# First block of a two-block network on one NeuronCore: raw products at the start of three stages, with the norm's root applied afterwards, and the state loaded in two parts

## The reference, cut to what matters

```python
def rms_norm(x, w):
    xf = x.astype(jnp.float32)
    y = xf * lax.rsqrt(jnp.mean(xf * xf, axis=-1, keepdims=True) + EPS)
    return (y * w.astype(jnp.float32)).astype(x.dtype)
def swiglu(x, w_gate, w_up, w_down):
    return (jax.nn.silu(x @ w_gate) * (x @ w_up)) @ w_down
```

## Time and profile before

| | |
|---|---|
| runs | 2658.94 us median of 3 (2658.17 to 2671.31) |
| the profiled execution | 2659.51 us |
| its span, first to last instruction | 2657.7 us |
| PE matmuls busy | 2567.2 us, 97% |
| PE weight loads busy | 2278.7 us, 86% |
| DVE busy | 1668.7 us, 63% |
| ACT busy | 1105.1 us, 42% |
| POOL busy | 66.1 us, 2% |
| DMA | 380.44 MB, mean 143 GB/s |

### The profile page before, as it was taken

The page is one execution under the profiler, slowest core; times in us unless marked ns, Lnnn a source line. Parts: engine busy times, 40 slices in busy tenths (PEclk is TensorE's granted clock), DMA queues, the critical chain, the costliest instruction groups (busy, mean ns, idle before and its releaser), DMA issues.

```text
span 2657.7 us, 38440 instructions
## 1 busy us (share of the span) xinstructions
PE 2567.2 (97%) x15728; PEld 2278.7 (86%) x15728; DVE 1668.7 (63%) x2629; ACT 1105.1 (42%) x1720; POOL 66.1 (2%) x60
## 2 busy tenths in 40 slices
PE   7998898999999999999999999999999999998998
PEld 7998798999888888778888888889888888888998
DVE  6767645777677665656644777655555446776655
ACT  5446654555322224444243422224222225655553
POOL 0001031000000000000000000000000000010000
PEclk9999999999999999999999999999999999999999
DMA  7775202675555543112222455553444423244554
GB/s 260 234 233 183 83 17 68 208 238 178 167 182 186 177 144 100 58 40 72 96 90 84 135 185 179 177 170 113 136 140 139 133 97 133 84 132 157 178 192 148
DMA packets 109536, 380.44 MB, mean 143 GB/s; under 512 B 11952, under 2 KB 15792, under 8 KB 108976
## 3 DMA queue, kind: packets, MB, share of 16 engines
q1 hardware_dynamic: 108352, 372.80, 42.6%
q10 hardware_dynamic: 1008, 5.18, 0.5%
HBM read 376.88 MB, written 1.05 MB: 142 GB/s over the span
## 4 chain that ended last, share of the span: by engine, by line
PE 89%; DVE 5%; ACT 3%; issue 2%; DMA 0%; SPq 0%; ACTq 0%; DVEq 0%
PE B L1497 26%; PE B L1498 25%; PE B L1499 25%; DVE w_lo L2126 2%; ACT w_hi L1819 1%; PE B L1758 1%; PE B L1741 1%; PE B L1512 1%; PE B L1651 1%; PE B L1513 1%; PE B L1664 1%; PE B L1514 1%; PE B L1748 1%; DVE AC L2371 1%; DVE TMP L2153 0%
## 5 line engine op out<-in xcount | busy, mean ns | idle before, releaser
L1497 PE MATMUL B<-U,w_hi 128*128 128x256 f32 (+1 forms) x2896 | 958.3, 331 | 7.7 <-DVE w_lo L2126 7.5
L1498 PE MATMUL B<-U,w_hi 128*128 128x256 f32 (+1 forms) x2896 | 950.1, 328 | 0.0
L1499 PE MATMUL B<-U,w_lo 128*128 128x256 f32 (+1 forms) x2896 | 950.0, 328 | 0.0
L2126 DVE TENSOR_TENSOR w_lo<-w_raw,w_hi 128x1024 fp32r<-128x1024 f32 (+3 forms) x583 | 683.6, 1185 | 391.9 <-ACT w_hi L1819 391.2
L1819 ACT ACTIVATE w_hi<-w_raw 128x1024 fp32r<-128x1024 f32 (+3 forms) x583 | 590.2, 1018 | 491.8 <-PE B L1499 470.4
L1497 PEld LDWEIGHTS B<-U,w_hi 128*128 128x128 f32 x2896 | 545.6, 188 | 64.3 <-issue 7.4
L1498 PEld LDWEIGHTS B<-U,w_hi 128*128 128x128 f32 x2896 | 545.5, 188 | 52.4 <-issue 1.5
L1499 PEld LDWEIGHTS B<-U,w_lo 128*128 128x128 f32 x2896 | 545.5, 188 | 51.9
L1497 PE MATMUL B<-HHf,w_hi 128*128 128x256 f32 (+1 forms) x1122 | 363.8, 324 | 1.7 <-DVE w_lo L2126 1.6
L1499 PE MATMUL B<-HHf,w_lo 128*128 128x256 f32 (+1 forms) x1122 | 362.9, 323 | 0.0
L1498 PE MATMUL B<-HLf,w_hi 128*128 128x256 f32 (+1 forms) x1122 | 362.9, 323 | 0.0
(11 more groups left out here) (355 smaller groups left out, 2537.9 us busy)
## 6 DMA issues: line engine op xcount, KB each, us to landing
w_raw<-in_w SPq DMA_DIRECT2D x504, 512.0 KB, 4.2
w_ada<-in_w SPq DMA_DIRECT2D x144, 512.0 KB, 3.3
w_raw<-in_w SPq DMA_DIRECT2D x58, 384.0 KB, 3.4
w_raw<-in_w SPq DMA_DIRECT2D x8, 320.0 KB, 2.8
X<-in_x SPq DMA_DIRECT2D x2, 1024.0 KB, 9.7
w_raw<-in_w SPq DMA_DIRECT2D x8, 256.0 KB, 2.7
BW<-in_bias ACTq DMA_DIRECT2D x1, 1536.0 KB, 10.3
K<-in_consts ACTq DMA_DIRECT2D x2, 640.0 KB, 4.5
```

The lines of the kernel that those rows point to most:

```text
L1497: pe.matmul(o, hi, xh, start=i == 0 and s.start, stop=False)
L1498: pe.matmul(o, hi, xl, start=False, stop=False)
L1499: e = pe.matmul(o, lo, xh, start=False, stop=i == last and s.stop)
L2126: dve.tensor_tensor(w_lo[:, plan.slot[u], 0:n], w_raw[:, plan.ring[u], 0:n], w_hi[:, plan.slot[u], 0:n].bitcast(F32), ALU.subtract).then_i ...
```

## The change

At the start of the three stages of the first block, four products instead of two are made side by side in two pairs, and they read `x w` without the root ("raw"). New step `raw`: ACT multiplies a tile of X by its gain into the high part, DVE makes the low part by one operation. It is done tile by tile as soon as the tile of X is final: after the load in the first FFN, after each `x_add` of the first FFN's down product for mixing, and after each `x_add1` of the output projection for the second FFN (in a new buffer `UR`; else in the free half of `U0`, `UO`). `raw_begin` then orders: the first half of the first pair (tiles 0 to 3, 24 matmuls), the sum over partitions and the root, the second half of the first pair (24), the second pair (48). The root comes in on evacuation: in `ffn_h` for columns 0 and 1 DVE multiplies the gate's product by r, ACT applies SiLU, DVE multiplies by r again and then by the up product; in `conv_in` for tiles 0 to 3 DVE multiplies by r while it copies. `norm_to_u` still makes the normalized state, which the next product (column tile 2 of an FFN; q0 in mixing) is the first to read. In `mix1`'s list, c2 and c3 move up behind c1. The state is loaded in two halves, with the first weight unit between them.

```diff
-                while done < min(at + AHEAD + 1, len(cut)) and (done < NH or cut[done - NH] in used):
+                while done < min(at + (s.n if s.kind == "fetch" and s.n else AHEAD + 1), len(cut)) and (done < NH or cut[done - NH] in used):
...
+    def raw_begin(self, name, view, keys, wts, stat):
+        need = tuple(("ul", ("raw", name, k)) for k in range(8))
+        b = [self.PS.get() for _ in range(4)]
+        f = dict(x=view, n=256, need=need)
+        self.add("pair", key=(), wts=wts[0][:8], b=b[0], b2=b[1], **f)
+        rb = stat.rsqrt(D)
+        self.add("pair", key=keys[:2], wts=wts[0][8:], k0=4, b=b[0], b2=b[1], **f)
+        self.add("pair", key=keys[2:], wts=wts[1], b=b[2], b2=b[3], **f)
+        return rb, dict(zip(keys, b))
...
-        order = "c0 c1 q0 q4 v b0 b1 o0 c2 c3 q1 q5 b2 b3 o1 c4 c5 c6 c7 s0 s1 q2 q6 b4 b5 o2 u0 u1 u2 u3 k0 k1 q3 q7 b6 b7 o3 c8 c9 c10 c11 s2 d w0 w1 g0 g1"
+        order = "c0 c1 c2 c3 q0 q4 v b0 b1 o0 q1 q5 b2 b3 o1 c4 c5 c6 c7 s0 s1 q2 q6 b4 b5 o2 u0 u1 u2 u3 k0 k1 q3 q7 b6 b7 o3 c8 c9 c10 c11 s2 d w0 w1 g0 g1"
...
+            elif k == "raw":
+                act.activation(HI[s.x][:, s.key[1], 0:256], X[:, s.key[1], 0:256], ACT.Copy,
+                               scale=col(*s.key)).then_inc(*up("uh", ("raw", *s.key)))
...
+            elif k == "raw":
+                dve.scalar_tensor_tensor(out=LO[s.x][:, s.key[1], 0:256], in0=X[:, s.key[1], 0:256], scalar=col(*s.key),
+                                         in1=HI[s.x][:, s.key[1], 0:256].bitcast(F32), op0=ALU.mult,
+                                         op1=ALU.subtract).then_inc(*up("ul", ("raw", *s.key)))
+            elif k == "conv_in" and s.rb:
+                dve.tensor_tensor(CV[:, s.key, 2:258], PS(s.b, 256), RB(s.rb, 256), ALU.mult).then_inc(*up("conv_r", s.key))
...
+                if s.rb:
+                    dve.tensor_tensor(h, PS(s.b, s.n), RB(s.rb, s.n), ALU.mult).then_inc(*up("g_r", s.key))
...
+                if s.rb:
+                    dve.tensor_tensor(h, h, RB(s.rb, s.n), ALU.mult).then_inc(*up("h_r", s.key))
...
-        sp.dma_start(X[:, :, 0:256], xs[:, :, 0:256]).then_inc(*landed("x", 0))
+        sp.dma_start(X[:, 0:4, 0:256], xs[:, 0:4, 0:256]).then_inc(*landed("x", 0))
         sp.dma_start(PC[:, 0:ncol], cols).then_inc(*landed("cols", 0))
+        weight_in(plan.cut[0])
+        sp.dma_start(X[:, 4:8, 0:256], xs[:, 4:8, 0:256]).then_inc(*landed("x1", 0))
+        weight_in(plan.cut[1])
         sp.dma_start(C1[:], consts[:, 0:256]).then_inc(*landed("c1", 0))
-        for u in plan.cut[:NR]:
-            sp.dma_start(w_raw[:, plan.ring[u], 0:plan.units[u][1]], source(u)).then_inc(*landed(f"w{plan.ring[u]}", u))
+        for u in plan.cut[2:NR]:
+            weight_in(u)
```

107 lines of the change are left out of this document (70 added, 37 removed).

## The result

| | before | changed |
|---|---|---|
| median of the runs | 2665.12 us of 4 | 2695.82 us of 4 (2691.30 to 2696.91) |
| ratio, 95% interval | | 1.0111 [1.0084, 1.0137] |
| profiled execution, its span | 2659.51, 2657.7 us | 2691.30, 2689.5 us |

The change costs 1.1%. In a second comparison it came out at 1.0096 [1.0059, 1.0133]. The forecast of 2674 had the sign right and the size at half, and the measured median lies outside its range of 2655 to 2685.

What follows compares the result with a forecast made beforehand. PE was taken to be nearly always busy, so only its stops and slow clock at the three stage starts could be won. 9.3 + 3 + 2.6 = 14.9 on 2659.5 gave 2674 us, range 2655 to 2685.

Steps and rivals of the forecast that it cites:

- the wait for `w_lo` in the value product: Sign of being right: in mixing, PE waits several us for the split's low part in the value product.
- First FFN, +9.3 forecast: Up product of column 3 starts at 46.5 instead of 37.2; +7.1 all at fast clock, +12.8 all slow.
- Mixing, +3 forecast: Value product ends at 237.2 where 233.2 is level, +4.0; 1 may come back behind; bounds -2 and +7.
- Three units from there, 8.2: Mixing: from the split of the value product's second unit at 229.0, three units take 8.2 us, to 237.2.
- my mark: Mixing: end of the value product, 227.76 before, taken as a point where PE runs without a stop again; level at 233.2.
- I have counted slow clock only in the first FFN: Clock assumption: slow products priced in the first FFN alone, none in the estimates for mixing or second FFN.
- Output projection and second FFN, +2.6 forecast: Column 3's up product in the second FFN starts at 488.2 against 485.65; bounds +0.5 and +5.3 (48 products slow).
- for two tiles and a split it then needs 3.3: Output projection: DVE needs 3.3 us where PE takes 2.7, so the second FFN's sum comes 1.2 late.
- The level case: Rival, chance 0.26, 2661 us: mixing bound by DVE and ACT chains, early taps give time back; mixing -5, first FFN +7.
- The faster case: Rival, chance 0.13, 2643 us: norm gets done under the second pair at all three places; -16.
- The rival of the clock that stays up: Rival, chance 0.12, 2672 us: pair products keep the clock through the sum; 7.1 + 3 + 2.6.
- The worse one: Rival, chance 0.07, 2688 us: POOL's stretch slows DVE's attention work, some 6 us over mixing's estimate, plus slow clock behind all norms.

Runs made afterwards that it cites:

- b4_parts: Kernel before with the state loaded in two parts, the first weight unit between them, no raw products: 2663.48 us, ratio 0.9990.
- c2_cb_early: Changed kernel with the loads of CN and CB right behind mixing's root, BW left behind the norm: 2694.35 us, ratio 1.0117.
- a2_after: The changed kernel once more, unchanged: 2689.16 us (4 runs, 2683.54 to 2702.67).
- a3_norm_second: Changed kernel with the second raw pair cut in two and the norm put between the halves: 2686.47 us, ratio 1.0081.
- a4_raw_f2: Kernel before with the state loaded in two parts, raw start in the second FFN alone, mixing's three loads issued later by oversight: 2680.58 us, ratio 1.0062.
- b1_load: Changed kernel with the three loads of mixing (CN, CB, BW) issued right behind the root: 2700.03 us, ratio 1.0129.
- b2_load_taps: Changed kernel with mixing's three loads behind the root and the taps of tiles 2 and 3 behind the first band: 2703.32 us, ratio 1.0139.
- b3_one_pair: Changed kernel with only each stage's first pair raw, norm right behind the root, mixing's loads early and taps late: 2695.67 us, ratio 1.0109.
- c3_squares_first: Changed kernel with the first FFN's squares ahead of the splits of the second and third weight unit: 2690.22 us, ratio 1.0103.
- c4_one_pair_mix: Kernel before with the state loaded in two parts and one raw pair in mixing alone, old order behind it: 2673.22 us, ratio 1.0036.
- d1_one_pair_cb: Kernel before with two-part load, one raw pair in mixing alone, and CN and CB loaded ahead of the norm: 2663.26 us, ratio 1.0002.
- d2_cb_taps: Changed kernel with CN and CB loaded behind mixing's root, BW behind the norm, taps of tiles 2 and 3 behind the first band: 2697.73 us, 1.0128.
- d3_after_copy: Changed kernel with POOL's eight mask additions replaced by copies of the mask, leaving out the position bias: 2688.72 us, ratio 1.0097.
- e1_cs_late: Changed kernel with the norm between halves of the second raw pair and CS moved behind two hidden tiles and column 3's split: 2696.31 us, 1.0109.
- a1_before: The kernel before once more, unchanged: 2664.19 us (10 runs, 2658.23 to 2676.56), ratio 0.9998.
- c1_stops: Kernel before with ten short PE stops added, at every fourth column tile of the first block's two FFNs: 2677.11 us, ratio 1.0054.
- d4_before_copy: Kernel before with POOL's eight mask additions replaced by copies of the mask, leaving out the position bias: 2662.49 us, ratio 1.0006.
- e2_stops_again: Kernel before with ten short PE stops added in the first block's two FFNs, run once more unchanged: 2679.76 us (one run).

## Why the prediction was wrong: right in sign, half in size

Forecast were 14.9 us, and the two profiled executions are 31.8 apart. Of the 16.9 that were missing, 11.5 are the long pitch, 5.6 mixing, and 2.7 the output projection and second FFN; the first FFN took 2.1 less than forecast, and 0.8 less came from elsewhere.

**Right.** The sums of mixing without a stop; the sum of the first FFN at 17.2 (I had 17 or 18); the wait at the first tile (1.04 to 1.15, I had 1.3) and over 2 us before the seventh, in the first FFN and in mixing; the load in two parts at nothing (b4_parts); slower. Not seen was the wait for `w_lo` in the value product: the one for `CB` stood in its place, and c2_cb_early, without that, has it (6.03).

**First FFN, +9.3 forecast, +7.2 at the mark.** 44.31 against 37.12. That is my bound with all of the second pair fast: the 1.93 us stop before the sums was not followed by slow products in this execution (in a2_after it was, and the mark came 1.7 later there). The load that gates the splits, which I had not counted, cost no more than the buffer, which I had.

**Mixing, +3 forecast, +8.6.** This is the term whose mechanism failed. Up to the split all came as forecast: behind the last residual addition the taps end at 29.9 us (I had 29.6) and the split of the value product's second unit at 31.0 (30.8). The step that failed is the next, "Three units from there, 8.2". It needs PE to be done with the first unit when that split is ready. But PE had stood still for 4.34 us for `CB`, started the first unit only at 241.01, ran more than half of it at the slow clock, and came to the second at 245.39, 2.6 us behind the split that was ready at 242.83. The three units from there took the 8.2. So the value product's end, my mark, was 6.8 late (its evacuation starts 42.0 us behind the last residual addition; level is 29.8 + 5.45), where I had 4. I had seen that the loads come later, and priced that for POOL alone; PE waited for `CB` of the same three. And I wrote "I have counted slow clock only in the first FFN", which put it at nothing here.

Behind the mark I had 1 us coming back, and 1.9 more were lost (3.7 in a2_after). Which wait does it stays open: PE's waits there are as long as before (23.0 and 22.8 us) and the time at the slow clock is 15.5 for 11.8, but b4_parts, with the old order in mixing, has 15.3 and is no slower for it. What the granted clock and the waits of the traces give for the whole stretch:

| run | stretch | PE's waits | time at 0.50 of the clock | 250.7 + more waits + half of the more slow time |
|---|---|---|---|---|
| before | 250.7 | 26.4 | 18.6 | |
| changed | 259.4 | 30.5 | 25.7 | 258.4 |
| a2_after | 260.4 | 30.5 | 30.1 | 260.6 |
| a3_norm_second | 255.6 | 29.4 | 21.6 | 255.2 |
| a4_raw_f2 | 254.5 | 28.9 | 25.8 | 256.8 |
| b1_load | 262.9 | 31.9 | 32.5 | 263.2 |
| b2_load_taps | 266.3 | 34.8 | 31.9 | 265.8 |
| b3_one_pair | 264.0 | 33.0 | 35.2 | 265.6 |
| c2_cb_early | 262.5 | 34.0 | 25.2 | 261.6 |
| c3_squares_first | 260.2 | 30.5 | 24.9 | 258.0 |
| c4_one_pair_mix | 255.8 | 30.7 | 21.4 | 256.4 |
| d1_one_pair_cb | 250.1 | 28.1 | 14.8 | 250.5 |
| d2_cb_taps | 261.9 | 31.8 | 31.6 | 262.6 |
| d3_after_copy | 258.9 | 28.6 | 29.3 | 258.3 |
| e1_cs_late | 260.7 | 30.5 | 28.3 | 259.7 |

The last column (half, since at 0.50 PE does half as much) meets the stretch within 2.3 us, from 250 to 266. Of the changed kernel's 8.6 us, 4.1 are waits and 3.6 are slow clock; of a2_after's 9.7, 4.1 and 5.8. PE either waits or works, so such a sum must come near: it says where the time went and not what caused it. It is no finer than 2 us either: the five other traces with the old order in mixing (a1_before, b4_parts, c1_stops, d4_before_copy, e2_stops_again) have stretches of 249.2 to 250.9 with 14.7 to 22.3 us of slow time, and it misses them by up to 1.7. That a stop can cost a slow stretch was in the earlier trace rows, and I had used it there, for what the change would win.

**Output projection and second FFN, +2.6 forecast.** 3.1 for the projection, and 2.2 behind it once the long pitch (5.2) is taken off its 7.4: 5.3, my upper bound, but not by what I had set for that bound: the slow time in the second FFN is 3.4 us in both kernels. The mis-sized step is "for two tiles and a split it then needs 3.3": it is 3.9, the distance from split to split, since DVE also stands still for ACT's rounding of every second raw tile. And the sums had a stop of 0.94 ahead where I had written that there is none.

```profile
477.29 1.22 DVE L2164 TENSOR_TENSOR w_lo<-w_raw,w_hi 128x1024 fp32r<-128x1024 f32 x1
...
480.44 0.48 DVE L2174 SCALAR_TENSOR_TENSOR URL<-X,PC,URH 128x256 fp32r<-128x256 f32 x1 [0.55 <-ACT URH L1897]
...
481.18 1.22 DVE L2164 TENSOR_TENSOR w_lo<-w_raw,w_hi 128x1024 fp32r<-128x1024 f32 x1
```

**The pitch, 0 forecast, 11.5 here.** I took each mark as "a point where PE is running without a stop again", and all behind it as the same. That failed, and by size it is the largest miss. Behind the mark PE still stopped for 0.3 us while splits caught up, and restarted at 0.1178. The kernel before can meet the long pitch too, so part of the 11.5 is luck of the two executions compared. The three times of the kernel before (2658.17, 2658.94, 2671.31) were in front of me; a gap of 13 us in a program that does the same each time should have made me ask what in it has two levels.

**The rivals.** The level case rested on taps done early paying back: b2_load_taps and d2_cb_taps show that where the taps stand only moves the wait. The faster case needed the norm under the second pair; a3_norm_second nearly had that in the first FFN, and the next chain took it. The rival of the clock that stays up had +7.1 for the first FFN, and 7.2 was measured, but by chance: PE did stop ahead of the sums, and behind the same stop the products were slow in a2_after. The worse one (2688) came close to the time by another road, pitch and the wait for `CB`; its mechanism, POOL, is about 1 us in the changed kernel.

## What to carry to other kernels

A stop of the matrix engine can cost a slow stretch behind it as well as itself: price both, also for the stops that a change adds. (The ten of c1_stops, 0.67 to 1.04 us idle each, had no slow stretch behind them; those of 2.53 and 2.12 us in the kernel before had.) Before work is moved ahead of a wait, list what else stands in that queue, loads above all, and who reads each of them first; then ask what is next in line at the same depth, since here load, taps, additions and band each took back what the one ahead had given. Trace the same order of work twice before you read a few microseconds from one trace. Where the times of an unchanged kernel gather in levels, find out what has the levels before comparing medians.

## What the runs showed of the hardware

- At a granted clock of 1.00, products 128x256 with a weight load each start every 0.1133 or every 0.1178 us, and a run of them keeps one of the two: some 1560 products in a row at the short one (before, first FFN), some 1480 at the long one (a1_before, second FFN); the exception stands above. The Trainium skill (TensorE: Matmul & The Clock Gate, "Wait — 56ns, not 53.3ns?") gives N / 2.4 GHz and about 2.5 ns for back-to-back matmuls, an estimate of 109.2 ns at 256 by that; neither pitch here is that, and the measured ones decide.
- The pitch changed at restarts, the last and next product 0.2 to 1.3 us apart, or differed from the moment when the clock came up (c1_stops short, e2_stops_again long): the same ten stops in two executions gave different sequences. What decides it stays open.
- POOL's addition and DVE's operations, each with two SBUF operands, slow each other: DVE's 0.48 to 1.21 us for 256 columns and 1.22 to 2.0 for 1024, POOL's 1.0 to 2.0. Beside a POOL copy DVE's 1.22 became 1.37 at most, and the copy's 0.51 became 1.5.
